# Sixteen more tokens of a PEER layer take their experts by gather, and the dense expert tables lose sixteen columns

## The reference, cut to what matters

```python
ug = jnp.take(u_table, eidx, axis=0)        # eidx: token x 8 heads x 16 experts
vg = jnp.take(v_table, eidx, axis=0)
hid = jnp.einsum('cd,chkd->chk', xc, ug)
a = jax.nn.gelu(hid, approximate=False) * g
return jnp.einsum('chk,chkd->cd', a.astype(vg.dtype), vg)
```

## Time and profile before

| | |
|---|---|
| median of 3 runs | 2504.95 us (2503.87 to 2505.03) |
| profiled execution, first to last instruction | 2502.2 us |
| PE busy | 2463.0 us, 98% |
| DVE busy | 1800.2 us, 72% |
| ACT busy | 1167.5 us, 47% |
| moved by DMA | 519.15 MB, mean 207 GB/s |

### The profile page before, as it was taken

The page is one execution under the profiler, slowest core; times in us unless marked ns, Lnnn a source line. Parts: engine busy times, 40 slices in busy tenths (PEclk is TensorE's granted clock), DMA queues, the critical chain, the costliest instruction groups (busy, mean ns, idle before and its releaser), DMA issues.

```text
span 2502.2 us, 35461 instructions
## 1 busy us (share of the span) xinstructions
PE 2463.0 (98%) x13593; PEld 2236.5 (89%) x13593; DVE 1800.2 (72%) x3332; ACT 1167.5 (47%) x1970; POOL 541.9 (22%) x344
## 2 busy tenths in 40 slices
PE   8999999999999999999999999999999999999998
PEld 7788888999999999999999999788788888888887
DVE  7876678998998886799888987777786335533323
ACT  6555466467767786333333335444422223422222
POOL 3222165133222342365544400000000000000000
PEclk9999999999999999999999999999999999999999
DMA  4211345588888999999999972222374223233231
GB/s 169 69 61 43 118 144 173 188 313 317 323 297 296 343 395 336 390 389 390 390 393 391 389 272 75 84 97 84 131 266 163 96 91 108 76 101 101 97 98 42
DMA packets 191239, 519.15 MB, mean 207 GB/s; under 512 B 15896, under 2 KB 67096, under 8 KB 187872
## 3 DMA queue, kind: packets, MB, share of 16 engines
q1 hardware_dynamic: 154208, 382.66, 43.1%
q0 software_dynamic: 36864, 134.23, 14.5%
HBM read 464.34 MB, written 52.49 MB: 207 GB/s over the span
## 4 chain that ended last, share of the span: by engine, by line
PE 92%; DVE 5%; ACT 1%; issue 1%; DMA 0%; POOL 0%; DVEq 0%; SPq 0%; ACTq 0%
PE P L1266 28%; PE P L1268 28%; PE P L1267 28%; PE P L1611 2%; PE P L1273 1%; DVE wl L1723 1%; DVE D L1723 1%; ACT wh L2370 0%; PE P L1544 0%; PE P L1543 0%; PE P L1542 0%; PE P L1522 0%; PE P L1521 0%; PE P L1524 0%; PE P L1520 0%
## 5 line engine op out<-in xcount | busy, mean ns | idle before, releaser
L1266 PE MATMUL P<-XH,wh 128*128 128x512 f32 (+2 forms) x2272 | 847.2, 373 | 7.5 <-DVE wl L1723 5.3
L1268 PE MATMUL P<-XH,wl 128*128 128x512 f32 (+2 forms) x2272 | 824.8, 363 | 0.0
L1267 PE MATMUL P<-XL,wh 128*128 128x512 f32 (+2 forms) x2272 | 823.9, 363 | 0.0
L2370 ACT ACTIVATE wh<-raw 128x1024 fp32r<-128x1024 f32 x458 | 482.4, 1056 | 347.5 <-PE P L1268 339.9
L1723 DVE TENSOR_TENSOR wl<-raw,wh 128x1024 fp32r<-128x1024 f32 x418 | 507.6, 1222 | 74.1 <-ACT wh L2370 73.9
L1266 PEld LDWEIGHTS P<-XH,wh 128*128 128x128 f32 x2272 | 428.8, 189 | 53.3 <-DVE wl L1723 7.8
L1268 PEld LDWEIGHTS P<-XH,wl 128*128 128x128 f32 x2272 | 427.6, 188 | 47.5
L1267 PEld LDWEIGHTS P<-XL,wh 128*128 128x128 f32 x2272 | 428.7, 189 | 42.5 <-issue 1.9
L1266 PE MATMUL P<-AH,wh 128*128 128x384 f32 x1024 | 343.4, 335 | 1.7 <-DVE wl L1723 1.7
L1268 PE MATMUL P<-AH,wl 128*128 128x384 f32 x1024 | 342.6, 335 | 0.0
L1267 PE MATMUL P<-AL,wh 128*128 128x384 f32 x1024 | 342.6, 335 | 0.0
(11 more groups left out here) (329 smaller groups left out, 3284.8 us busy)
## 6 DMA issues: line engine op xcount, KB each, us to landing
raw<-wts SPq DMA_DIRECT2D x211, 512.0 KB, 3.6
raw<-ut SPq DMA_DIRECT2D x128, 512.0 KB, 6.6
raw<-vt SPq DMA_DIRECT2D x128, 512.0 KB, 12.1
hdram<-HID SPq DMA_DIRECT2D x64, 384.0 KB, 4.7
gdram<-GS SPq DMA_DIRECT2D x24, 1024.0 KB, 6.4
GI<-gdram SPq DMA_DIRECT2D x16, 1536.0 KB, 16.5
HI<-hdram SPq DMA_DIRECT2D x32, 768.0 KB, 16.7
AWC<-adat SPq DMA_DIRECT2D x64, 256.0 KB, 5.0
```

The source lines that it names most:

```text
L1266: e.matmul(bank, wh[:, w], H, start=start, stop=False)
L1267: e.matmul(bank, wh[:, w], L, start=False, stop=False)
L1268: return e.matmul(bank, wl[:, w], H, start=False, stop=stop)
L2370: return e.activation(dst, src, ACT.Copy)
```

## The change

`NX = 16` tokens (0 to 15) leave the dense way, so every dense tile has 368 columns and there are 92 gate steps (`STEPS`). Their 16 x 8 heads are laid over 128 partitions, so that 16 more gather steps do for each table: 132 `dot` steps in stage U (`NU`), 144 `axpy` steps in stage V. The new steps multiply by `XF`, the 16 token vectors each repeated on eight partitions (16 transposes on PE, two copies on ACT, two adds on DVE, and a way through DRAM), and add into `SUMF`. At the end one matmul of 16 columns per bank (`TOK`) sums the eight partitions of a token. The costs in the timeline change: 2.85 to 2.55 for a `dot`, 6.2 to 5.6 for an `axpy`, and others. Reading back is also changed: `HI` has five buffers of two tiles in place of two of four tiles, each is issued six units ahead of its use, and `GI` has issues of its own, also six units ahead (four before).

```diff
+NX = 16
+NDD = ND - NX
+STEPS = NDD // 4
+NU = 128 - LATE + NX
...
             yield ("dot", s)
-            yield 2.85
+            yield 2.55
...
-            yield 1.6 if n % 2 and n > 2 else 3.1
-            due += 3.0 if n < 32 else 4.0
+            yield 1.5 if n % 2 and n > 2 else 2.9
+            due += 3.1 if n < 32 else 4.1
...
-            dots_due += 1.2 if n < 30 else 1.0 if n < 62 else 1.4
+            dots_due += 1.4 if n < 28 else 1.2 if n < 58 else 1.65
...
-        for s in range(LATE + 128):
-            if s + 5 < LATE + 128:
+        for s in range(LATE + 128 + NX):
+            if s + 5 < LATE + 128 + NX:
                 yield ("gather_v", s + 5)
...
-            yield 6.2
+            yield 5.6
...
 def activate(i):
-    if i % 4 == 0 and i // 4 + 1 < 32:
-        yield ("fetch", i // 4 + 1)
+    if i % 8 == 2 and i // 8 + 1 < 16:
+        yield ("fetch_gates", i // 8 + 1)
+    if i % 2 == 0 and i // 2 + 3 < 64:
+        yield ("fetch", i // 2 + 3)
...
-                    t = product(P[k][:, 0:ND], u, k, AH[i % 4][:, :], AL[i % 4][:, :], i == 0, i == 127)
+                    t = product(P[k][:, NX:ND], u, k, AH[i % 4][:, :], AL[i % 4][:, :], i == 0, i == 127)
...
+            def few_turn(n):
+                if n == 0:
+                    p.wait_ge(s_keyc, 16)
+                else:
+                    p.wait_ge(s_fcopy, was_fill + n)
+                part = (XH, XL)[n % 2]
+                for c in range(4):
+                    t = e.transpose(P[5][:, 128 * c:128 * c + 128], part[:, 4 * (n // 2) + c, 0:128].bitcast(F32), ident[:, :])
+                t.then_inc(s_fturn, 1)
...
             def rows_turn(d):
-                p.wait_ge(s_rows, rows_done(LATE + 127))
-                e.transpose(P[d][:, ND:T], SUM[:, 128 * d:128 * d + 128], ident[:, :]).then_inc(s_y, 1)
+                w = slice(128 * d, 128 * d + 128)
+                p.wait_ge(s_rows, rows_done(LATE + 127 + NX))
+                e.transpose(P[d][:, ND:T], SUM[:, w], ident[:, :])
+                e.matmul(P[d][:, 0:NX], SUMF[:, w], TOK[:, :], start=True, stop=True).then_inc(s_y, 1)
```

More of the change, by code:

```diff
@@ L406, in dots @@
             yield ("gather", s)
-        for s in range(128 - LATE):
-            if s + 3 < 128 - LATE:
+        for s in range(NU):
+            if s + 3 < NU:
                 yield ("gather", s + 3)
             yield ("dot", s)
-            yield 2.85
+            yield 2.55
         yield ("dots_end", 0)
@@ L505, in background @@
         more, due, dots_due = iter(()), 0.0, 0.0
[L506 to L509, removed]
+        yield ("few_spread",)
+        for n in range(STEPS + 2):
+            q = n + Q0
+            if n == 0 or q == 32:
+                more, due = route_more(q // 32 + 1), 0.0
+            if q in (30, 62):
                 for piece in more:
                     yield piece
-                yield ("gate_turn", n // 32 + 1)
+                yield ("gate_turn", q // 32 + 1)
+            if 34 <= q < 38:
+                yield ("few_turn", q - 34)
+            if q in (40, 42):
+                yield ("few_cast", q // 2 - 20)
             if n % 2 and n > 2:
@@ L529, in background @@
                     due -= piece
[L530 removed]
+            dots_due += 1.4 if n < 28 else 1.2 if n < 58 else 1.65
             yield from some(int(dots_due))
             dots_due -= int(dots_due)
[L533 removed]
+        yield from some(NU)
     for i in range(128):
@@ L537, in timeline @@
             yield from side.rest()
-            yield ("fetch", 0)
+            yield ("fetch_gates", 0)
+            for n in range(3):
+                yield ("fetch", n)
         yield from group(U_U + i)
@@ L870, in build_program @@
         IOP = at("IOP", F + 84.25, [128, 16, 2], F16)
-        HID = [at(f"HID{i}", F + 84.75 + 3 * i, [128, 2, ND], F32) for i in range(2)]
+        HID = [at(f"HID{i}", F + 84.75 + 3 * i, [128, 2, NDD], F32) for i in range(2)]
         XT = at("XT", F + 90.75, [128, 1024], F32)
@@ L1079, in row_count_v @@
         def row_count_v(s):
-            return s // 6 + 1 + (len(range(s % 6, 128 - LATE, 4)) if s % 6 < 4 else 0)
+            return s // 6 + 1 + (len(range(s % 6, NU, 4)) if s % 6 < 4 else 0)
         def rows_done(r):
-            return 1 + 128 - LATE + 1 + r + 1 + (r >= LATE)
+            return 1 + NU + 1 + r + 1 + (r >= LATE)
         def wh_of(u):
@@ L1704, in _ @@
             work = {f.__name__: f for f in (
-                tile, tile_half, v_turn, scores, turn, values, key, token, rows, rows_turn, gate_turn, grid, warm, ones2, first_ones,
+                tile, tile_half, v_turn, scores, turn, values, key, token, rows, few_turn, rows_turn, gate_turn, grid, warm, ones2, first_ones,
                 r_turn, r_scores, r_values, r_root, down)}
@@ L2547, in rows, with few_turn @@
                 copy(XT[:, 512 * half:512 * half + 512], P[6][:, :]).then_inc(s_sc, 1)
+            def few_turn(n):
+                if n % 2 == 0:
+                    w = slice(512 * (n // 2), 512 * (n // 2) + 512)
+                    c.wait_ge(s_pairs, 24)
+                    c.wait_ge(s_fturn, was_fox + n + 1)
+                    copy(XF[0:NX, w], P[5][0:NX, :]).then_inc(s_fcopy, 1)
             def dots_end(part):
                 w = slice(128 - LATE, 128) if part else slice(0, 128 - LATE)
-                c.wait_ge(s_rows, rows_done(LATE - 1) if part else 129 - LATE)
+                c.wait_ge(s_rows, rows_done(LATE - 1) if part else 1 + NU)
+                if part == 0:
+                    e.activation(HSF[:, :], HSF[:, :], ACT.Gelu)
                 e.activation(HS[:, w], HS[:, w], ACT.Gelu).then_inc(s_gexp, 1)
```

179 lines of the change are left out of this document (120 added, 59 removed).

## The result

The changed kernel takes 2522.0 us (median of 4 runs, 2519.7 to 2525.2) against 2504.4: a ratio of 1.0071, 95% interval 1.0058 to 1.0084. It is slower by 17.6 us, where 12 us faster was forecast.

A forecast was written before the change was run, and what follows sets the result against it. PE's own stream was taken as the bound, with DMA within 2% in stage V. Of a 39.1 us ceiling, stage U keeps 9 and stage V 3, so 2504.9 - 12 = 2493 us; forecast's range 2480 to 2499, overall 2466 to 2514.

The forecast's parts named there:

- The saving of 16 columns: Dense matmuls on PE: 16 fewer columns save 6.5 ns each, 40.0 us over 6144 matmuls, half in each stage.
- the weight load is no floor: Dense matmuls on PE: weight loads do not limit the narrower tiles; the opposite, zero saving, got chance 0.02.
- stage V would be bound by bytes: Stage V: eight units move 13.20 MB, 33.8 us at 390 GB/s against PE's 31.95, so 1.9 us late.
- Three signs that were named: Profile after: ACT's raw waits well over 8 us, DVE over 95% busy mid-stage U, GB waits growing over 15 us.
- rival 3: Last third of stage U: longer landings in the ring of four GB buffers make it slower, 2515 or 2525; chance 0.18.
- Part is absorbed once ... I estimate 10 us: Stage V: buffers standing ahead absorb 10 us (between 0 and 19) of 25.6 us lateness; PE loses 16 of 19.
- It is 5 to 8 late; ... I take 5: Last third of stage U: transfers take 149 to 152 us against PE's 144; 5 us lost after wl buffers absorb part.
- rate and ring: Last third of stage U: 152 us by bytes at 410 GB/s, 149 us by four buffers with 9.0 us landings.
- the threshold of L = 9.8: Last third of stage U: gather landing time in us from which the four-buffer ring decides, costing 17 us.
- I allow 3 us: Middle of stage U: ten more dots make DVE 98% full in fixed order, costing 3 us (0 to 8).
- Rival 1: Transfers keep up, so nearly the whole ceiling comes: 2466, or about 2472 with stage U's losses; chance 0.18.
- the ceiling of 39 us: PE's whole saving if always fed: 40.0 + 1.9 - 1.8 - 1.0 = 39.1 us, 20.1 in stage U, 19.0 in V.

The follow-up runs named there:

- e3: Changed kernel with each gate load reading one contiguous piece per partition instead of 23 pieces of 512 bytes (gates in wrong order): 2497.6 us, ratio 0.9975.
- e9: Changed kernel with six GB buffers instead of four from dot 76 on: 2510.2 us, ratio 1.0025.
- e1: Changed kernel without 15 of the 16 added gather steps for each table, with the spacings of before: 2481.0 us, ratio 0.9905.
- e4: Changed kernel making only the first four gathers in stage U, dots then using stale rows: 2502.9 us, ratio 0.9996.
- The three repairs: Changed kernel with gates written in small and read in long pieces, six GB buffers from dot 76, old gate-step and routing spacings: 2482.8 us, ratio 0.9922.
- e12: Kernel before the change with gates written in small pieces and read in long ones: 2504.0 us, ratio 0.9999.
- e5: Changed kernel with the gate loads issued by ACT's queue instead of SP's: 2574.7 us, ratio 1.0278.
- e7: Changed kernel with gates written in 512-byte pieces and read in one contiguous piece per partition: 2493.8 us, ratio 0.9956.

## Why the prediction was wrong

**Right.** The saving of 16 columns, 6.5 ns: over 1080 to 1400 us PE has 1848 matmuls before and, where it never waits, 1922 in e3, 173.3 and 166.6 ns. So the weight load is no floor, though PEld is busy 320.00 of 320 us in both. The Trainium skill (Perfetto Trace Analysis, Identifying the Most-Contended Engine) judges the headroom by the busy share of LDWEIGHTS, and by the matmul FLOPs done against the peak beside it; the first of the two would have allowed no gain at all here. The window of the kernel before, against that of e3 above:

```profile
1080.00:1400.00 320.00, 320.00 (x1848) 320.00 (x1847) 287.12 (x335) 119.57 (x156) 170.27 (x101) 1.00 1.05 390
```

Right too: stage V would be bound by bytes: 13.20 MB at 390 GB/s were to take 33.8 us, and 33.9 were measured; and a gate load's slow pieces are what keeps 410 from 390. Three signs that were named came: ACT's waits for `raw` well over 8 us, DVE over 95% busy in the middle (325.6 of 340 us), and, for rival 3, DVE's waits for `GB` in the last third, 20 us against 2.9 in the whole of stage U before. The ring of four buffers was at work, though not by longer landings. The ceiling of 435 GB/s of the Trainium skill (DMA: Bandwidth & Descriptors, Where 436 GB/s comes from) was reached in no run: 411 over 320 us and 416 over 26 us (e9, 836 to 862) are the best. The same section says that for transfers from DRAM a limit of about 358 GB/s for each core binds instead; 390 and 411 here, on one core, are above it.

**The step that failed first: "Part is absorbed once ... I estimate 10 us".** In stage V PE was to lose 16 of its 19 us. By PE's starts units 8 to 112 went from 432.6 to 440.0, 7.4 us longer, where the sum without any cushion gives 13 x (33.8 - 33.2) = 8 (the 12.6 of the first table has in it that ACT in the kernel before got further ahead of PE over these units). The cushion was worth nothing. The first 24 units of stage V did run at or near PE's pace (32.0, 32.6 and 32.0 us for eight), and the next eight took 37.9: what was saved came back at once, with a lower clock behind it. The next stalls come at every second gate load (1.8 us up to 1207 us, 3.3 up to 1274), later ones less regularly; why every second is open. Stage V as a whole, from U 127 to V 120, lost 10 us where 3 were to be gained; by PE's starts it is 11.1 us longer to its end. Ten us of that miss are the cushion, and most of the rest is the wait for the positions behind the last gather, which has no term in the sum.

**The second: the last third of stage U, "It is 5 to 8 late; ... I take 5".** It is 193.8 us against 176 at PE's pace (e1: 175.2, e4: 174.2), 18 late. I had put it down to rate and ring as two readings of one number, at a steady landing of 9.0 us. The landing did stay there (minimum, median and maximum 5.1, 9.1 and 11.4 us, 830 to 970 us), so the threshold of L = 9.8 in rival 3 was the wrong test. Dots come in pairs, and the gate steps' `OM` and the weights' `wl` stand between, so the time of a full turn is paid now and then in whole, and PE then restarts slowly; with six buffers most of it was gone (179.7).

**The third: the middle, "I allow 3 us".** The ideal was 24 to 88 in 283 us (292.6 less 1536 x 6.5 ns); it took 289.7, and 283.8 with the old spacings. I had costed the dots and not the compressed gate steps and routing, which were the cause: DVE was late above all at the second gate transposition.

**The sum.** Units 0 to 24 gained nothing, where the forecast had left 1. By stretch the forecast of -12 was -1 (0 to 24), -6.5 (24 to 88), -1.5 (88 to 127) and -3 (from there to V 120), measured were +0.9, -2.9, +10.8 and +10.2: 2, 4, 12 and 13 us off, 31 in all, as by the profiled execution; by the medians it is 2522 - 2493 = 29.

Rival 1's 2466 is the ceiling of 39 us. The three repairs reach 2483, so 17 us of it stay out of reach here; e1, which asks for fewer gathers, has 2481.

## What to carry to other kernels

A stage in which no engine waits can be without reserve in its transfers, and the DMA share does not tell: it was 1.05 before, where 390 GB/s was also the most that this traffic could have, and 0.99 in e12, where 388 were moved and 411 could be had (e3). Work out bytes per period against the rate that starved stages measured, and take no cushion off a deficit that lasts longer than the buffers. Before adding transfers look at the shape of those that are there; pieces of 512 bytes on the read side cost 1.8 us in each 34 (33.8 against 32.0 by PE's starts), and moving them to the write, in stage U, made the change pay. Where a fixed order feeds a ring of buffers, cost the ring by its worst turn, and try more buffers before blaming the rate.

## What had not been expected of the hardware

A stall of PE can cost twice: after one of 4.4 us that ended at 1140 the granted clock was 0.57 over the next 4 us, and over 320 us of stage V it was 0.98, where PE that never waited kept 1.00. Not every stall did so: the one that ended at 1207, of 1.8 us, had 1.00 behind it.

The load of 512-byte pieces took up to 36 us on a queue of its own, against at most 26.6 among SP's other loads, and the whole rate fell from 390 to 340 GB/s (e5): on a queue of its own the slow load became slower.

```profile
1080.00:1400.00 320.00, 276.48 (x1562) 274.56 (x1561) 247.29 (x289) 95.83 (x130) 178.44 (x94) 0.93 0.92 340
```

Stores in 512-byte pieces, all of them in stage U (e7, e12), showed no cost that could be measured, where loads in such pieces held the rate at 390 instead of 411 GB/s.
